# Decoder step on one Trainium2 core: four of eight output parts summed in PSUM over the whole expert loop, the other four through two banks

## The reference

```
h    = rms_norm(x)                     # (T, 1024)
q    = h @ w_query                     # 8 heads; scores against two sets of 128 keys
gate = softmax(top 16 scores)          # per head; expert = e1 * 128 + e2
act  = gelu(expert_u[eid] . h)
y    = sum over chosen experts of gate * act * expert_v[eid]
x    = x + y;  out = rms_norm(x)
```

## Time and profile before

| | |
|---|---|
| median of 3 runs | 2084.02 us (2077.91 to 2084.51) |
| the profiled execution | 2084.53 us, its span 2082.7 us |
| TensorE busy / weight load | 1977.2 us (95%) / 1696.2 us |
| VectorE / ScalarE / GpSimd busy | 1414.6 us (68%) / 622.9 us / 463.7 us |
| mean granted clock of TensorE | 0.935 of full speed |

### The profile page before, as it was taken

How to read it: one execution, slowest core, us unless ns; L and a number is a source line. 1 busy time by engine, 2 the same in 40 slices (tenths; PEclk the granted TensorE clock), 3 DMA queues, 4 the chain that set the end, 5 groups by cost and what they waited for, 6 DMA issues and landing times. The chain is left out here.

```text
span 2082.7 us, 28113 instructions
## 1 busy us (share of the span) xinstructions
PE 1977.2 (95%) x9593; PEld 1696.2 (81%) x9593; DVE 1414.6 (68%) x3185; ACT 622.9 (30%) x1032; POOL 463.7 (22%) x598
## 2 busy tenths in 40 slices
PE   7999999999999998998799999999999999998994
PEld 5886567774567764787699999999999999998993
DVE  2356333311399997877678887888888888785773
ACT  1221322201211113666233233333333333322332
POOL 0000740000023322000333443433333333320000
PEclk9999557769999999999899999999999999999996
DMA  8010402111322112554888988898988888874542
GB/s 337 3 51 18 188 1 87 66 42 55 115 72 71 61 43 70 209 215 175 299 276 264 308 302 279 303 310 269 319 290 276 309 299 288 268 257 144 162 134 100
DMA packets 195776, 381.93 MB, mean 183 GB/s; under 512 B 13167, under 2 KB 134957, under 8 KB 192269
## 3 DMA queue, kind: packets, MB, share of 16 engines
q1 hardware_dynamic: 157733, 243.52, 34.6%
q0 software_dynamic: 36864, 134.23, 18.3%
q10 hardware_dynamic: 1056, 2.62, 0.3%
HBM read 343.51 MB, written 35.34 MB: 182 GB/s over the span
## 5 line engine op out<-in xcount | busy, mean ns | idle before, releaser
L1277 PE MATMUL bank<-p_high,v_high 128*128 128x416 f32 x896 | 317.0, 354 | 9.5 <-DVE v_low L1687 5.0
L1277 PE MATMUL bank<-p_high,v_low 128*128 128x416 f32 x896 | 318.0, 355 | 0.0
L1277 PE MATMUL bank<-p_low,v_high 128*128 128x416 f32 x896 | 314.8, 351 | 0.0
L1229 PE MATMUL bank<-h_high,u_high 128*128 128x416 f32 x768 | 271.8, 354 | 20.5 <-DVE u_low L1687 19.8
L1229 PE MATMUL bank<-h_high,u_low 128*128 128x416 f32 x768 | 272.2, 354 | 0.0
L1229 PE MATMUL bank<-h_low,u_high 128*128 128x416 f32 x768 | 269.7, 351 | 0.0
L1458 POOL DMA_INDIRECT rows<-in_u_rows,row_u x128 | 172.5, 1347 | 259.8 <-DVE dots L1769 198.4
L1387 ACT CAST p_high<-gel 128x416 fp32r<-128x416 f32 x128 | 69.2, 540 | 492.2 <-DVE gel L1732 488.3
L1458 POOL DMA_INDIRECT rows<-in_v,row_u x128 | 148.6, 1161 | 293.2 <-DVE y L1764 226.8
L453 PE MATMUL proj<-w_in_sb,xT 128*128 128x256 f32 (+1 forms) x880 | 193.7, 382 | 15.6 <-DVE xT L331 12.4
L453 PEld LDWEIGHTS proj<-w_in_sb,xT 128*128 128x128 f32 (+1 forms) x880 | 154.0, 176 | 53.6 <-DVE xT L331 12.4
(11 more groups left out here) (212 smaller groups left out, 3085.4 us busy)
## 6 DMA issues: line engine op xcount, KB each, us to landing
vv<-in_v SPq DMA_DIRECT2D x112, 512.0 KB
u<-in_uT SPq DMA_DIRECT2D x96, 512.0 KB
gates_kept<-staged SPq DMA_DIRECT2D x13, 2048.0 KB, 7.5
gate<-gates_kept SPq DMA_DIRECT2D x30, 832.0 KB
early<-in_uT SPq DMA_DIRECT2D x32, 512.0 KB, 3.5
w_in_sb<-in_w_in SPq DMA_DIRECT2D x4, 2048.0 KB, 22.1
wq<-in_w_q SPq DMA_DIRECT2D x16, 512.0 KB, 3.5
u<-in_v SPq DMA_DIRECT2D x16, 512.0 KB
```

Source lines behind the costliest of these rows:

```text
L1229: ins = pe.matmul(a_ps[par][:, 0:DT], x[:, par, k], y, start=(k == 0 and n == 0), stop=(k == KT - 1 and n == 2))
L1277: ins = pe.matmul(y_ps[m % 4][:, 0:DT], x[:, c, at:at + P], y, start=(c == 0 and n == 0), stop=(c == CG - 1 and n == 2))
```

## The change

Parts 0 to 3 of y (`KEPT` = 4) each get a bank of their own, 0 to 3, into which all 32 groups are summed: only the first matmul of the first group opens the sum, only the last of the last group closes it. They are copied to SBUF once, at the end (`take_kept`). Parts 4 to 7 rotate through banks 4 and 5 and are still added to `yT` on DVE after each group; `weigh` waits for the add of the part two back in that sequence. The step order, the loads and all other waits are as before.

```diff
+KEPT = 4
...
-        y_ps, a_ps, g_ps = banks[0:4], banks[6:8], banks[0:4]
+        kept_ps, y_ps, a_ps, g_ps = banks[0:KEPT], banks[KEPT:6], banks[6:8], banks[0:4]
+        SUMMED = KT - KEPT
...
             def weigh(part, gg, m):
                 g = GROUPS * part + gg
-                q = KT * g + m
...
-                wait(pe, y_added, q - 3)
+                if m >= KEPT:
+                    wait(pe, y_added, SUMMED * g + m - KEPT - 1)
+                known = isinstance(part, int)
+                opens = m >= KEPT or known and part == gg == 0
+                closes = m >= KEPT or known and (part, gg) == (PARTS - 1, GROUPS - 1)
+                out = (y_ps[m % 2] if m >= KEPT else kept_ps[m])[:, 0:DT]
...
-                        ins = pe.matmul(y_ps[m % 4][:, 0:DT], x[:, c, at:at + P], y,
-                                        start=(c == 0 and n == 0), stop=(c == CG - 1 and n == 2))
+                        ins = pe.matmul(out, x[:, c, at:at + P], y, start=(opens and c == 0 and n == 0),
+                                        stop=(closes and c == CG - 1 and n == 2))
...
-            nc.gpsimd.memset(yT[:, :, P:T], 0.0).then_inc(y_zero, 1)
+            nc.gpsimd.memset(yT[:, KEPT:KT, P:T], 0.0).then_inc(y_zero, 1)
...
             def add(part, gg, m):
-                q = KT * (GROUPS * part + gg) + m
-                wait(dve, y_added, q - KT + 1)
-                dve.wait_ge(v_done, q + 1)
+                if m < KEPT:
+                    return
+                g = GROUPS * part + gg
+                wait(dve, y_added, SUMMED * (g - 1) + m - KEPT + 1)
+                dve.wait_ge(v_done, KT * g + m + 1)
                 acc = yT[:, m, P:T]
-                nc.vector.tensor_tensor(acc, acc, y_ps[m % 4][:, 0:DT], ALU.add).then_inc(y_added, 1)
+                nc.vector.tensor_tensor(acc, acc, y_ps[m % 2][:, 0:DT], ALU.add).then_inc(y_added, 1)
+
+            def take_kept(m):
+                dve.wait_ge(v_done, KT * (NG - 1) + m + 1)
+                nc.vector.tensor_copy(yT[:, m, P:T], kept_ps[m][:, 0:DT])
...
-            for m in range(KT):
+            for m in range(KEPT):
+                take_kept(m)
+            for m in range(KEPT, KT):
                 add(PARTS - 1, GROUPS - 1, m)
```

## The result

The changed kernel takes 2092.55 us (5 runs, 2091.04 to 2095.57) for 2084.02 (5 runs, 2077.91 to 2087.39). The ratio is 1.005, 95% interval 1.0029 to 1.007: slower by about half a per cent, 5 us above my 2087.5 and inside the range. The outcome I had held likeliest, within 0.3%, did not come; slower had 0.32. The profiled execution took 2092.34 us with a span of 2090.6, 7.9 above the span before.

The account below looks back on a forecast made before the run. TensorE's own stream of matmuls was taken to bound the loop, so only its idle time could change. The terms -5.0 + 6.5 + 2.0 gave +3.5 us, a median of 2087.5 us, with a range of 2079.5 to 2095.

Parts of the forecast that it names:

- the relief: VectorE, in each group: four adds fewer, 2.0 us a group, of which 5.0 us was to reach the end.
- adds removed: Expert loop: VectorE's dropped adds end most of TensorE's 6.1 us idle from 1026 to 1762; -5.0 us, bounds 2 and 6.1.
- new wait inside parts 0 to 5: (g, 6) waits for add 4 of its own group instead of add 2; costed at nothing.
- new wait at the entry, and the clock: Entry of part 6: (23, 6) and (24, 6) wait for late adds, +6.5 us; TensorE at half clock, +2.0 us.
- steady groups 25 to 30: Late groups: add 4 comes early enough for (g, 6), with 0.5 us to spare; no cost.
- the rest: Matmuls adding into open banks, four copies at the end, smaller memset: nothing, within half a microsecond either way.
- Two banks too few in all late groups: Rival for parts 6 and 7: 1.5 us lost in each of groups 25 to 30, 9.1 us, giving 2096.6; chance 0.12.
- The relief wins: Rival: all 6.1 us of TensorE idle return and the entry stall costs nothing, giving 2077.9; chance 0.1.
- Nothing moves: Rival: VectorE's head start is lost at every landing and the entry stall is short, giving 2084; chance 0.13.

Follow-up runs that it names:

- spread: The changed kernel with 184 counting instructions on TensorE among the matmuls of weigh in part 0; 2083.67 us for 2082.41 of the kernel before.
- late_spread: `four_banks_late` with 184 counting instructions on TensorE among the matmuls of weigh in part 0; 2075.03 us for 2082.06 of the kernel before, ratio 0.9969.
- again: The changed kernel measured once more, the same program; 2091.82 us for 2084.2 of the kernel before, ratio 1.0032.
- padded: The changed kernel with an idle wait ahead of each kept part, making the loop bodies longer; 2093.79 us for 2083.93 of the kernel before.
- shifted: The changed kernel with 48 TensorE instructions ahead of the loop that only count up an unused counter; 2094.36 us, ratio 1.004.
- add_first: The changed kernel with adds 4 and 5 moved ahead of step w4 in the groups without activations; 2088.86 us, ratio 1.0015.
- four_banks_late: The changed kernel, but from group 23 on parts 4 to 7 take four banks, two from the ended activations; 2082.17 us for 2084.2 of the kernel before.
- waits_alone: The kernel before with all eight adds kept, but with the banks and waits of the change; 2104.41 us, ratio 1.0095.
- late_shifted: `four_banks_late` with 48 TensorE instructions ahead of the loop that only count up an unused counter; 2080.89 us, ratio 0.9973.
- before_shifted: The kernel before with 197 TensorE instructions ahead of the loop that only count up an unused counter; 2103.95 us, ratio 1.0078.
- two_kept: The changed kernel with two parts kept instead of four, six parts rotating through four banks, two adds less a group; 2086.35 us, ratio 1.0.

## Why the prediction was right or wrong

The time was in the range and the sign right, but the relief was much too small and one cost was missing. The two errors, -4.2 and +7.4 us, partly cancelled: that the time stayed inside the range was in part luck, though the entry was forecast link by link. The starts in `spread` and in the changed kernel give all terms (in us):

| step | forecast | measured |
|---|---|---|
| adds removed | -5.0 | -9.2 up to (23, 4) in spread |
| new wait inside parts 0 to 5 | 0 | 0: no wait for an add before 1860 |
| new wait at the entry, and the clock | +6.5 + 2.0 | +9.1 after, +9.7 in spread |
| steady groups 25 to 30 | 0 | +0.1 |
| the rest | 0 | **+7.4**: (23, 4) at -1.7 after, -9.2 in spread |
| sum | +3.5 | +7.5 by starts, 7.9 by spans |

**Adds removed: the term was mis-sized.** I capped it at the 6.1 us idle from 1026 to 1762. Of those only some 2.7 to 3.3 us came back by (20, 0), so my doubt about late landings was sound (3.4 us of waits for u splits stay in `late_spread`). The rest lay where I had not looked: one wait for a v split behind 1762, with half a clock after it, worth about 3.5 us between (20, 0) and (22, 6). The kernel before has it,

```profile
1774.53 0.56 PE L1277 MATMUL bank<-p_high,v_high 128*128 128x416 f32 x1 [1.75 <-DVE v_low L1687]
```

and the windows of 1762 to 1780 show it, first the kernel before, then after:

```profile
1762.00:1780.00 18.00, 16.25 (x79) 15.62 (x78) 13.15 (x15) 4.96 (x7) 4.63 (x5) 0.91 0.79 282
```

```profile
1762.00:1780.00 18.00, 18.00 (x97) 17.83 (x97) 14.89 (x17) 5.07 (x7) 5.89 (x7) 1.00 0.95 341
```

Another 2.3 to 2.9 us came between (22, 6) and (23, 4), where the kernel before has a stretch at 1.2 GHz that neither kernel has after. I had given the relief nothing behind 1762.

**The entry: right, link by link.** (23, 6) lost 4.8 us against (23, 4) (`again` 4.8, `spread` 4.7), forecast 4.7. From the split of (24, 1) at 1907.57 to (24, 6) at 1922.06 are 14.49 us, forecast 14.5. Between them the clock came in, for 2.4 us and not as an extra stretch beside the stall: the matmuls of (23, 6) and (23, 7) ran at 1.2 GHz behind the long idle (they are those from 1895.22; a matmul row there is 0.68 long for 0.35), so (23, 7) ended later, and piece (24, 1) was loaded later. 4.8 + 2.4 + 1.9 = 9.1 for 8.5. The granted clock of the 70 us is 0.95 in both kernels, so the halved time only moved to where it delays a load. The Trainium skill ("TensorE: Matmul & The Clock Gate", "HAM oscillation") has each burst of matmuls behind a long wait for DMA begin at the lower clock. Here the wait is for an add: the burst behind the 6.84 us does so, that behind the 2.36 us ahead of (24, 6) does not, as the 0.95 over 70 us is 7 us at the lower level, and the first burst takes that up; in `padded` and `shifted` there are 3.4 us at 1.2 GHz at (24, 6) too. `add_first` and `four_banks_late` confirm that the wait for the add was the price: half of it gone gave 3 to 4 us, all of it about 10 (9.4 by the starts at (31, 6)).

**Steady groups: right**, with the reason tested: without the relief, `waits_alone`, it is 1.6 us a group.

**The rest, at nothing: wrong.** This is the step that failed. I had listed matmuls, copies and the memset, and not the program. The change takes 56 instructions from TensorE's compiled program (17024 to 16968), most of them in the loops, where they served the waits of the kept parts; its second loop ends at 52.98 packets in place of 53.14, and the second pass is fetched again: 75 packets for 66, 8.5 us lost at once, of which about 1 was given back by idle time that it hid; net 7.4 us, by `spread` against after (5.9 against `again`). In medians less the kernel before of the same session it is worth 6 to 7 us (+8.5 and +7.6 us with it, +1.3 in `spread`), in the medians as they stand 8 to 9 (2083.67 for 2091.82 and 2092.55); the entry is worth about 9 either way (2075.03 for 2083.67). Not every pair agrees as well: `late_shifted`, with the second fetch, has the ratio 0.9973 and `late_spread`, without it, 0.9969, though their starts at (31, 6) lie 8.1 us apart.

That the second fetch and the idle go together, and that adding instructions outside the loops moves both from one loop to the other or takes them away, is shown. What they cost is shown for the changed kernels to some 2 us; in `before_shifted` it was nothing in the end. Why a place brings it is not shown: I suppose that the fetch ahead has by then overwritten the loop's head, but no row shows which part of the program is held. The kernel before, too, has a packet start 7.2 us ahead of its back edge and is not fetched again, and `two_kept` and `padded` differ in outcome with the same ends, so the supposition is incomplete at best.

**The rivals.** Two banks too few in all late groups: not so, for the reason given. "The relief wins" gave the relief 6.1 us for the 9.2 measured and the entry nothing for 9.1. "Nothing moves" is what `spread` came to, by cancelling and not for the rival's reason: -9.2 and +9.8.

## What to carry to other kernels

Count where a new wait stands in the order of every engine, and follow the load behind it: the entry of part 6, some 30 us of 2090, cost as much as the adds of 32 groups had won. Give back the resource where it is free again: the activations' banks from group 23 on turned +0.3% to +0.5% into +0.1% to -0.3%. And when an engine waits for nothing that the profile shows, at a loop's back edge, compare the packets of the instruction queue; a loop of TensorE can be fetched again after an edit that only moves it, and an A/B test of the edit then measures the move too. Look at the other engines' back edges as well.

## What the runs showed of the hardware

- A loop body of 6.3 packets of 256 instructions ran its second pass without a fetch in 66-packet programs: in the kernel before the queue q8 brings nothing from 1256 to 1426 us and from 1567 to 1739. In the programs with 75 and 76 packets the second pass of one loop is fetched like straight code, three packets in the first 10 us or so and then one about each 24 us, and TensorE stands 3 to 7 us at its start.
- Instructions that only count a semaphore are not free in a row: TensorE stood 31.21 us at 197 of them ahead of the loop and 8.19 us at 48, 0.16 to 0.17 us each, and was at 1.2 GHz behind the 197, while the 184 among the matmuls of part 0 cost nothing (from (0, 0) to (4, 0) TensorE's starts went from -0.3 to -0.7 us against before in `late_spread`).
- In the changed kernel an idle time of 6.8 us was followed by 6.8 us at 1.2 GHz, one of 3.6 us at the back edge by 10.2 us, one of 2.4 us ahead of (24, 6) by none there and by 3.4 us in `padded` and `shifted`.
- The other instruction queue, q14, brings three packets of 8 KB within about 7 us at one of the two back edges in each kernel here, and VectorE stood there without a releaser for 0.6 us in the kernel before, 3.2 in the changed one and 6.2 in `two_kept`.
